# Expert rows gathered as two picks of 64 tokens, weighed on half of TensorE's columns, and in side-by-side pairs in the second half

## The reference, cut to what matters

```
top_s, top_i = lax.top_k(sub_scores, 16)          # twice 128 sub-keys per head
fin_s, fin_pos = lax.top_k(cand_s, 16)            # of 256 sums
gates = softmax(fin_s)
u_sel = take(u, expert)                           # [token, pick, 1024]
act = gelu(einsum('chkd,cd->chk', u_sel, h)) * gates
out = einsum('chk,chkd->cd', act, take(v, expert))
x = x + out                                       # then rms_norm, and block 2:
x = x + 0.5 * swiglu(x);  x = x + mixer(x);  x = x + 0.5 * swiglu(x)
```

## Time and profile before

| | |
|---|---|
| median of 3 runs | 3600.69 us (3599.6 to 3603.47) |
| span of the profiled execution | 3601.5 us |
| PE, weight loads, DVE, ACT, POOL busy | 92%, 73%, 71%, 43%, 21% of the span |
| PE matmul records, DVE, ACT instructions | 18706, 4532, 3089 |
| HBM traffic | 908 MB read, 8 MB written, 254 GB/s over the span |
| indirect DMA (picks) | 537 MB; slabs and the rest by hardware queues: 379 MB |

### The profile page before, as it was taken

One profiled execution on the slowest core, in us unless ns is written; L12 is line 12 of the kernel. 1 busy time (PEld: TensorE's weight loads), 2 busy tenths in 40 slices (PEclk: granted clock), 3 DMA queues, 4 the chain that ended last, 5 costly groups with the idle time before them and its releaser, 6 DMA issues.

```text
span 3601.5 us, 50492 instructions
## 1 busy us (share of the span) xinstructions
PE 3316.3 (92%) x18706; PEld 2633.5 (73%) x18706; DVE 2554.4 (71%) x4532; ACT 1537.0 (43%) x3089; POOL 770.5 (21%) x577
## 2 busy tenths in 40 slices
PE   7998889979898777799999999989999999999998
PEld 6886669855463222688777777767899988998898
DVE  6997143676777877687767777877867576768665
ACT  3222234245443333454444444545445443444443
POOL 1001236123435666122122122222200000000000
PEclk9999999999999999899899999999999999999999
DMA  3332224569999999699888899879956844453455
GB/s 123 94 95 75 75 83 141 182 272 397 407 415 421 417 411 418 261 377 389 324 321 312 305 372 385 317 296 341 374 176 188 267 141 131 133 184 106 140 184 156
DMA packets 184174, 918.82 MB, mean 255 GB/s; under 512 B 21536, under 2 KB 26912, under 8 KB 118128
## 3 DMA queue, kind: packets, MB, share of 16 engines
q0 software_dynamic: 73728, 536.90, 37.4%
q1 hardware_dynamic: 99248, 358.66, 29.9%
q10 hardware_dynamic: 10960, 20.12, 1.8%
HBM read 907.80 MB, written 7.80 MB: 254 GB/s over the span
## 4 chain that ended last, share of the span: by engine, by line
PE 72%; DVE 9%; DMA 7%; issue 5%; ACT 4%; POOL 2%; ACTq 0%; DVEq 0%; POOLq 0%
PE psum L715 54%; PE psum L1068 11%; DMA buffer_float<-in_peer_uv,buffer_uint 7%; DVE buffer_bfloat L2578 2%; POOL buffer_float L3259 2%; PE psum L1289 1%; ACT slabs_rounded L1452 1%; PE psum L723 1%; DVE buffer_float32r L2185 1%; PE psum L1274 1%; DVE norm_recip_root L2193 1%; DVE slabs_remainder L2279 1%; PE psum L1286 1%; PE psum L1372 1%; PE psum L1336 1%
## 5 line engine op out<-in xcount | busy, mean ns | idle before, releaser
L715 PE MATMUL psum<-buffer_float32r,slabs_rounded 128*128 128x256 f32 (+2 forms) x9568 | 2005.4, 309 | 70.3 <-POOL slabs_remainder L3244 30.1
L715 PEld LDWEIGHTS psum<-buffer_float32r,slabs_rounded 128*128 128x128 f32 x9568 | 1556.1, 192 | 217.3 <-issue 113.5
L715 PE MATMUL psum<-buffer_float32r,slabs_remainder 128*128 128x256 f32 (+2 forms) x4784 | 1439.8, 301 | 0.0
L2279 DVE TENSOR_TENSOR slabs_remainder<-raw_slabs,slabs_rounded 128x1024 fp32r<-128x1024 f32 x601 | 732.8, 1223 | 452.2 <-ACT slabs_rounded L1452 434.1
L1452 ACT ACTIVATE slabs_rounded<-raw_slabs 128x1024 fp32r<-128x1024 f32 x662 | 695.7, 1055 | 698.5 <-PE psum L715 620.7
L1068 PE MATMUL psum<-buffer_float,buffer_float 128*128 128x512 f32 x1712 | 825.2, 612 | 137.8 <-ACT buffer_float L1753 124.5
L715 PEld LDWEIGHTS psum<-buffer_float32r,slabs_remainder 128*128 128x128 f32 x4784 | 918.1, 192 | 29.8
L3259 POOL DMA_INDIRECT buffer_float<-in_peer_uv,buffer_uint x512 | 623.2, 1217 | 1330.8 <-PE psum L1068 753.6
L2578 DVE CUSTOM_DVE_ANT_0 buffer_bfloat<-buffer_float,buffer_float 128x1024 bf16<-128x1024 f32 x512 | 625.3, 1221 | 169.5 <-DMA buffer_float<-in_peer_uv,buffer_uint 160.8
L1068 PEld LDWEIGHTS psum<-buffer_float,buffer_float 128*128 128x128 f32 x1712 | 304.3, 193 | 519.6 <-issue 509.7
L1742 ACT ACTIVATE buffer_float<-buffer_float 128x1 f32<-128x1 f32 x512 | 100.3, 196 | 368.5 <-DVE buffer_float L2578 366.6
(11 more groups left out here) (213 smaller groups left out, 2039.0 us busy)
## 6 DMA issues: line engine op xcount, KB each, us to landing
raw_slabs<-in_slabs SPq DMA_DIRECT2D x682, 512.0 KB
buffer_float<-in_peer_uv,buffer_uint POOLq DMA_INDIRECT x512
buffer_float<-kept ACTq DMA_DIRECT2D x4, 874.5 KB, 6.0
xT<-in_xT ACTq DMA_DIRECT2D x4, 512.0 KB, 5.7
buffer_float<-in_consts ACTq DMA_DIRECT2D x8, 256.0 KB
kept<-buffer_float ACTq DMA_DIRECT2D x4, 512.0 KB
buffer_float<-kept ACTq DMA_DIRECT2D x2, 875.0 KB, 6.7
kept<-buffer_float ACTq DMA_DIRECT2D x4, 272.0 KB
```

Source lines behind the costliest of these rows:

```text
L715: m = pe.matmul(out, a, b, start=start and j == 0, stop=stop and j == 2)
L2279: dve.tensor_tensor(slab_l[:, r, :], raw[:, r, :], slab_h[:, j, :].bitcast(F32), ALU.subtract)\
```

## The change

A gather tile now holds **two picks of 64 tokens** in place of one pick of 128: the lower 64 partitions have one pick of a group's 64 tokens, the upper 64 another of the same tokens. There are 8 groups of 64 gathers. `eidx` and `gates` are written in that layout, with four instructions in place of one each. The token rows `hrow[g]` hold the 64 tokens' rows twice. For groups 0 and 1 ACT writes them from the banks (`twin_rows`); the rows of token tiles 1 to 3 are written to DRAM (`rows_d`) and each group's are loaded from there by two DMAs of 256 KB on ACT's queue (`load_rows`), for groups 2 and 3 when groups 0 and 1 are done, for 4 and 5 at pick 192, for 6 and 7 when groups 4 and 5 are done. DVE waits for them before a group's first dot.

The diagonal becomes a 128 x 64 matrix (two 64 x 64 identities on top of each other, scaled), so a matmul sums both picks into 64 partitions. Alternate gathers go to partitions 0 to 63 and 64 to 127 of the banks. In the first half each is weighed by itself; in the woven half PE weighs two at a time, the matmul on the lower columns followed at once by that on the upper ones. `turn_rows` multiplies `out_rows` with the stacked identity, which adds both halves and transposes. It is called 8 times in place of 4, into one bank each, and `take_sums`, `add_sums` and the hold of three slabs come once a group: `TURN` has 62, 117, 170 and 229. PE's `added_by` takes t-2 in place of t-3. `by_dve` has 80 of the woven picks in place of 84, PE 176 in place of 172.

```diff
 def turn_after(n):
-    return next(t for t in range(BLOCK2) if woven_by(t - 3) >= n)
-TURN = (turn_after(PICKS), turn_after(WOVEN))
-def added_by(t, behind=3):
-    n = woven_by(t - behind)
-    return PICKS if n > PICKS and t < TURN[0] + 3 else n
+    return next(t for t in range(BLOCK2) if woven_by(t - 2) >= n)
+BOUNDS = [GROUP * (j + 1) for j in range(WOVEN // GROUP)]
+TURN = [turn_after(n) for n in BOUNDS]
+def held(n, t):
+    for bound, turn in zip(BOUNDS, TURN):
+        if n > bound and t < turn + 3:
+            return bound
+    return n
+def added_by(t, behind=2):
+    return held(woven_by(t - behind), t)
 def by_dve(n):
-    return n >= PURE and n % PICKS % 3 == 2
+    return n >= PURE and n % GROUP % 3 == 2 and n % GROUP < GROUP - 2
...
-        diag = part(SLOTS, P)
+        diag = part(SLOTS, H64)
...
-            def weigh(n):
-                slot, turn, p = n % SLOTS, n // SLOTS, n % PICKS
-                pe.wait_ge(uv_landed[slot], 16 * turn + 16)
-                pe.wait_ge(diag_done, DIAGONALS[n + 1])
-                for q in range(2):
-                    m = pe.matmul(psum[:, b, :], diag[:, slot, :], uv_rows[slot][:, D + q * 512:D + (q + 1) * 512],
+            def weigh(*picks):
+                for n in picks:
+                    pe.wait_ge(uv_landed[n % SLOTS], 16 * (n // SLOTS) + 16)
+                pe.wait_ge(diag_done, DIAGONALS[picks[-1] + 1])
+                for q in range(2):
+                    for n in picks:
+                        g, slot, j = n // GROUP, n % SLOTS, DIAGONALS[n] % 2
+                        m = pe.matmul(psum[j * H64:(j + 1) * H64, b, :], diag[:, slot, :],
+                                      uv_rows[slot][:, D + q * 512:D + (q + 1) * 512], start=first, stop=last)
...
             def weigh_to(n):
                 while woven[0] < n:
                     if not by_dve(PURE + woven[0]):
-                        weigh(PURE + woven[0])
+                        waiting.append(PURE + woven[0])
                     woven[0] += 1
+                    if len(waiting) == 2:
+                        weigh(*waiting)
+                        waiting.clear()
...
+            def twin_rows():
+                for q in range(2):
+                    b = full(at.take())
+                    for g in range(2):
+                        for c in range(2):
+                            m = act.activation(hrow[g][c * H64:(c + 1) * H64, q * 512:(q + 1) * 512],
+                                               psum[g * H64:(g + 1) * H64, b, :], ACT.Copy)
...
+            def load_rows(g):
+                t, s = g // 2 - 1, g % 2
+                for c in range(2):
+                    act.dma_start(hrow[g][c * H64:(c + 1) * H64, :], rows_d[t, s * H64:(s + 1) * H64, :])\
+                        .then_inc(rows_here[s], 16)
...
-                step(dve.tensor_copy(eidx[:, tt, h0 * TOPK:h1 * TOPK], pk.fin_af[:, some].rearrange("p a b -> p (a b)")))
+                two = pk.fin_af[:, some].rearrange("p h (i c) -> p c (h i)", c=2)
+                for s in range(2):
+                    for c in range(2):
+                        step(dve.tensor_copy(eidx[c * H64:(c + 1) * H64, 2 * tt + s, h0 * TOPK // 2:h1 * TOPK // 2],
+                                             two[s * H64:(s + 1) * H64, c]))
```

More of the change, by code:

```diff
@@ L234 @@
     DIAGONALS.append(DIAGONALS[-1] + (not by_dve(_n)))
-assert not any(by_dve(tt * PICKS + p) for tt in range(QT) for p in (0, PICKS - 1))
+assert all(DIAGONALS[g * GROUP] % 2 == 0 for g in range(GROUPS + 1))
 def score_pieces(h):
@@ L1087, in _, with turn_rows @@
+            def turn_rows(sums, bn):
+                for b, n in sums:
+                    pe.wait_ge(bank_free[b], n + 2)
+                pe.wait_ge(bank_free[bn[0]], bn[1] + 1)
+                for k in range(KT):
+                    m = pe.matmul(psum[:, bn[0], k * H64:(k + 1) * H64], out_rows[:, k * P:(k + 1) * P], stacked,
+                                  start=True, stop=True)
+                m.then_inc(bank_full[bn[0]], 1)
+            last_sums = None
             steps = second_half()
@@ L1745, in coefficient @@
                 act.wait_ge(gelu_done, n + 1)
-                act.activation(coefs[:, slot:slot + 1], acts[:, slot:slot + 1], ACT.Copy, scale=gates[:, tt, p:p + 1])\
+                gate = gates[:, n // GROUP, n % GROUP:n % GROUP + 1]
+                act.activation(coefs[:, slot:slot + 1], acts[:, slot:slot + 1], ACT.Copy, scale=gate)\
                     .then_inc(coef_done, 1)
@@ L1752, in coefficient, with take_sums @@
                 act.wait_ge(coef_done, n + 1)
-                act.activation(diag[:, slot, :], ident[:, :], ACT.Copy, scale=coefs[:, slot:slot + 1])\
+                act.activation(diag[:, slot, :], stacked, ACT.Copy, scale=coefs[:, slot:slot + 1])\
                     .then_inc(diag_done, 1)
-            def take_sums(tt, sums, turned):
+                g = n // GROUP + 2
+                if n % GROUP == GROUP - 1 and g < GROUPS and g not in (QT, QT + 1):
+                    if g == 2:
+                        act.wait_ge(rows_kept, 16)
+                    load_rows(g)
+            def take_sums(g, sums, turned):
+                if turned:
+                    full(turned)
                 for q in range(2):
@@ L1770, in _ @@
             turned = None
-            for tt in range(2):
-                sums = [acc.take(), acc.take()]
-                for p in range(PICKS):
-                    n = tt * PICKS + p
-                    coefficient(n)
-                    if n - STEP_LAG in STEPS:
-                        next(steps)
-                    if n in GATE_PICK:
-                        gate_exps(GATE_PICK[n])
-                take_sums(tt, sums, turned)
-                turned = [at.take(), at.take()]
+            for n in range(PURE):
+                if n % GROUP == 0:
+                    sums = [acc.take(), acc.take()]
+                coefficient(n)
+                if n - STEP_LAG in STEPS:
+                    next(steps)
+                if n in GATE_PICK:
+                    gate_exps(GATE_PICK[n])
+                if n > GROUP and n % GROUP == TURN_AT + STEP_LAG:
+                    turned = at.take()
+                if n == LATE_ROWS:
+                    act.wait_ge(rows_kept, 16 * (QT - 1))
+                    load_rows(QT)
+                    load_rows(QT + 1)
+                if n % GROUP == GROUP - 1:
+                    take_sums(n // GROUP, sums, turned)
+            turned = at.take()
             assert next(steps, None) is None
@@ L2068, in stream_squares @@
             def stream_squares(h, dst):
-                for bn in turned:
-                    emptied(bn)
+                emptied(turned)
                 for k in range(KT):
@@ L2571, in dot @@
             def dot(n):
-                tt, p = divmod(n, PICKS)
-                slot, turn = n % SLOTS, n // SLOTS
+                slot, turn, g = n % SLOTS, n // SLOTS, n // GROUP
+                if n % GROUP == 0 and g > 1:
+                    dve.wait_ge(rows_here[g % 2], 32 * (g // 2))
                 dve.wait_ge(uv_landed[slot], 16 * turn + 16)
@@ L2716, in _ @@
                     make_gates(GATE_PICK[n - 7])
-                if p == PICKS - 1:
-                    turned = [at.take(), at.take()]
+                if n > GROUP and n % GROUP == TURN_AT + STEP_LAG:
+                    turned = at.take()
+            turned = at.take()
             assert next(choosing, None) is None and next(steps, None) is None
-            add_rows(1, turned)
+            add_rows(QT - 1, turned)
             sums = [acc.take(), acc.take()]
-            place, woven, added = [0], [0], [0]
+            place, woven, added, turned_at = [0], [0], [0], [None]
             def add_row(n):
@@ L2739, in _, with add_sums @@
             last_row = [0]
[L2741 removed]
+            def add_sums(g, sums):
                 before = last_row[0]
```

164 lines of the change are left out of this document (85 added, 79 removed).

## The result

The changed kernel takes **3628.04 us** (median of 4 runs, 3619.58 to 3634.8) against 3601.32 (4 runs, 3599.6 to 3603.47). The ratio is 1.0079, interval 1.0063 to 1.0094: **slower by 27 us**. I had forecast 3554, and 3628 is above the top of the range, 3610.

What follows compares the result with a forecast made beforehand. DMA bounds the first picks and PE the woven half; terms -12 - 3 - 7 - 40 + 2 + 8 + 1 + 1 + 2.5 = -47.5 us from 3601.5 give 3554 us, range 3500 to 3610.

Steps and rivals of the forecast that it cites:

- the column halves: Woven half: matmuls on two column halves overlap, a pair taking 1.92 us against 3.44; at most 127 us given back.
- the first half: First 256 picks: costs of 8 us for traffic, 1 us for group ends and 2.5 us for choosing.
- traffic: Token rows to DRAM and back on ACT's queue: 8 us lost in the first picks, 1 us in the woven half.
- choosing: Extra DVE copies and gate products before the first gathers: 2.5 us lost, bounds 1.5 and 5.
- holds: Woven half: three holds at group ends at 2 us each, 6 in place of 4, so 2 us lost.
- the SwiGLUs: First SwiGLU 12 us gained plus 3 in its down part, second 7 us, with DMA becoming the limit.
- One slab sooner: Woven half, PE asking for coefficients a slab earlier: waits up to 0.6 us at every other pair, no separate cost.
- the thirds left out: First SwiGLU, up and gate: two thirds, 12 of 18 us, counted as gain; the rest was to cover waits.
- the mixer: Mixer: 72 us of PE relief at most, 55% of it, 40 us, taken as gain; bounds 15 and 72.
- The clock: First picks: with half the array in use the clock could fall to 1.2 GHz, costing over 100 us; chance 0.03.
- The first rival: Woven half: pairs overlap but time reappears as waits on landings, DVE and ACT; 3590 us (3580 to 3605), chance 0.11.
- The slower rival: Every pair of the woven half: the column halves do not overlap, 3641 us; chance 0.15.

Runs made afterwards that it cites:

- e10: The changed kernel with PE's lag of two slabs in the mixer and three in the two SwiGLUs: 3610.75 us, ratio 1.0030.
- e12: First 256 picks whole with rows in SBUF as in the kernel before, pairs in the woven half alone, e10's lag: 3592.11 us, ratio 0.9979.
- e9: The changed kernel without the rows' writes to DRAM, their loads and DVE's waits for them: 3614.29 us, ratio 1.0036.
- e2: The changed kernel with the lag of before, three slabs in place of two: 3612.4 us, ratio 1.0032.
- e8: The kernel before with two more holds of three slabs, at the 64th and 192nd woven pick, no other work: 3604.01 us, ratio 1.0008.
- e3: The changed kernel with holds of two slabs in place of three: 3635.15 us, ratio 1.0101.
- e13: e12 with the mixer's extra picks one in six slabs in place of one in five: 3563.26 us, ratio 0.9901.
- e4: The kernel before with only the lag shortened, PE asking for picks of two slabs ago: 3666.86 us, ratio 1.0178.
- e7: The changed kernel with the lag of three slabs and every pick weighed by itself on its column half: 3668.92 us, ratio 1.0190.
- the hybrid: The kernel of e12, first 256 picks as before and pairs in the woven half alone: 3592.11 us; at the slower pace it is e13, 3563.26 us.
- the better hybrid: The kernel of e13, e12 with the mixer's extra picks one in six slabs: 3563.26 us, ratio 0.9901.

## Why the prediction was wrong, point by point

**Right: the column halves.** A pair takes 1.87 us behind a slab and 1.94 behind a wait, forecast 1.92. The toll is a little larger than put, since 0.18 more shows in the slab behind: PE is given back 296 - 88 x 2.05 = 116 us, not 127. The Trainium skill's page cited there, TensorEngine Tiling (Array Packing), section Key Properties, has both halves of it: the tiles run in parallel, and the change of mode drains TensorE. The trace agrees, with 8 passes in 1.94 us, and has 0.32 us for going over and back, for which the page has no figure.

**Right in kind, low by some 7 us: the first half.** I had 8 of traffic, 1 of group ends and 2.5 of choosing, 11.5 in all; e10 against e12 says 19. Traffic is 14 (the dots of e9 against the median of the changed first halves, and its time). Choosing is more than 2.5 too. POOL's wait for the gates, 63.5 us in the earlier trace rows, became 68.2:

```profile
POOL buffer_float L3326 <- DVEq L2632: 68.2, 1, 68.2
```

and the first dot came 1.3 us later in this execution and 3.2 in e2, and in the median of all profiles with this choosing 4 us later than in those with the old. In all, the 256th dot starts 18 us later in the median than with the first half of before. The sum for one head was low: the four copies take 0.76 us where the one took 0.17, 0.59 more against the 0.27 put. I took 0.09 us a copy from a pair on 128 partitions in the earlier trace rows; in the chain after, the copies on 64 partitions take 0.13 to 0.18 each, and start 0.16 to 0.19 apart:

```profile
746.31 0.13 DVE buffer_uint L2597
...
746.47 0.17 DVE buffer_uint L2597
...
746.66 0.18 DVE buffer_uint L2597
```

**Right as far as tested: holds.** 2 us forecast, 2 measured for the two added in e8, at the old lag and with whole picks; the shorter holds of e3 brought nothing. No run tests the turning by itself.

**Right with the old lag: the SwiGLUs.** I had 15 for the first. It is 238 to 228 in e2 and in e13, 10 us, with DMA at 407 GB/s as the new limit, as forecast. In e13 the cut of the second goes from 156 to 143 us, 13 where I had 7, and the whole of it, four picks more included, from 264 to 254.

**The step that failed: "One slab sooner", costed at nothing of its own.** I closed that sum inside ACT: 2.8 to 3.6 us of turn against 3.0 of slab, with a wait of up to 0.6. I did not ask when ACT's turn can begin. It begins with a rounding that needs a slab to have landed, and that load is released by PE itself three slabs earlier. The sum to make was 7.5 to 9.9 us of landing, 1.06 of rounding, 1.0 to the diagonal with gaps, 9.6 to 12.0 us, against three slabs of 3.0 with what is woven between them. The earlier trace rows even had the sign, 9.0 us of waiting for slabs in 24 of them; I read it as room for DMA and not as the far side of PE's own wait. The price was not a wait of up to 0.6 us at every other pair, hidden in the thirds left out: in e4 the step costs 65 us, and in the changed kernel 16; by the profiles 24 are lost in the two SwiGLUs and 13 gained in the mixer. The loop is seen in the first SwiGLU (17 us in e4, 16 in the changed kernel) and not in the mixer. Why the mixer loses 48 us with whole picks and gains with pairs is open.

**The larger miss, in a term that was mis-sized: the mixer, 40 us forecast with bounds 15 and 72.** It was 1 in the changed kernel and 13 the wrong way at the old lag. I had kept 55% of the relief as if PE's other waits grew by no more than the rest; in e2 against e7 52 of 102 us went to new idle time of PE and about 41 to slower matmuls, at a lower clock. The clock I had put to the first picks alone as a rival (there it read 0.96 to 0.99 from 1100 to 1400 us in six profiles of this layout, 0.99 to 1.00 in three of the old one; PE is not the bound there) and never to the stage where PE is relieved. With the slower pace the hybrid gets 23 us, inside the bounds.

The first rival, "the picks were not what held it", named this mechanism (time reappearing as waits on landings, DVE and ACT) and gave it 0.11; its price, 3590, left no room for a loss. The slower rival had the wrong place: I looked for a loss in the new instruction and not in the lag.

The 74 us between forecast and result are then 16 for the lag, 7 for the first half, and about 51 for relief in the woven half that did not come through. The mixer is the largest part of it, and its cause is known only as far as the idle time and the clock.

**What stays open.** How the mixer's loss divides between landings, the order of ACT and DVE, and the clock: they feed each other, and no run here holds one of them fixed. What holds ACT in the mixer when the lag is shortened. Why the slower pace brings 29 us in the hybrid, 21 in the changed kernel and 4 at a lag of 3. The pairs' kernels also scatter more from run to run, 3599.7 to 3622.2 in e10 against 3599.6 to 3603.5 before, so that single profiles of them are poor witnesses for less than some 10 us.

## What to carry to other kernels

A lag between an engine and its supplier is a buffer over everything in the loop behind it, so before taking one step out of it, follow the chain backwards from the wait to the event that released the first transfer, and sum the whole loop against the work between. Then check it stage by stage, since the same lag can cost in one stage and pay in another. Relief of the bounding engine is worth what the next loop lets through: here 116 us of it gave 8 us with the first half as before and the lag restored in the stages near the DMA ceiling, and 36 when the pace of the picks was lowered too. Where a layout serves only one stage, put it into that stage alone: 19 of the 65 us between the changed kernel and the better hybrid are its price in the first half.

## What was not expected of the hardware

- Changing between the whole array and column halves shows on both sides: 0.14 us in the pick and 0.18 us in the slab behind it, in which 24 matmuls took 3.19 us in place of 3.01.
- With less work on PE its clock was lower: over the mixer's stretch the mean granted clock was 0.96 with singles (e7) and 0.91 with pairs (e2), and some 41 of 102 us of relief came back as slower matmuls. In e13 pairs have 0.95, so it is not the work alone.
- The rows' traffic cost more than its bytes: from 1100 to 1400 us all queues together moved 401 to 407 GB/s with it, 415 without it (e9) and 415 to 417 with the first half of before, and between the first dot and the 256th it took 701 - 687 = 14 us where the bytes make 8.
- Copies of DVE on 64 partitions started 0.16 to 0.19 us apart, where the second of a pair on all partitions took 0.09 us.
